# Two more weight slots for the experts, and their bias rows loaded later on the queue

## The reference

```python
def expert_block(args):
    xe, e = args
    gate = jnp.minimum(xe @ w_gate[e] + b_gate[e], SWIGLU_LIMIT)
    up = jnp.clip(xe @ w_up[e] + b_up[e], -SWIGLU_LIMIT, SWIGLU_LIMIT)
    act = (up + 1) * (gate * jax.nn.sigmoid(SWIGLU_ALPHA * gate))
    return act @ w_down[e] + b_down[e]
...
y = yb[dest] * sorted_w[:, None].astype(h.dtype)
return jax.ops.segment_sum(y, sorted_tok, num_segments=t)
```

## Time and profile before

| | us |
|---|---|
| median of three runs | 1945.78 |
| the three runs | 1941.55, 1945.78, 1946.54 |
| the profiled execution | 1945.98 |
| its span | 1944.1 |
| TensorE busy in it | 1815.6 (93%) |
| VectorE busy | 770.6 (40%) |
| ScalarE busy | 601.6 (31%) |

### The profile page before, as it was taken

The page is one execution under the profiler, slowest core; times in us unless marked ns, Lnnn a source line. Parts: engine busy times, 40 slices in busy tenths (PEclk is TensorE's granted clock), DMA queues, the critical chain, the costliest instruction groups (busy, mean ns, idle before and its releaser), DMA issues.

```text
span 1944.1 us, 24816 instructions
## 1 busy us (share of the span) xinstructions
PE 1815.6 (93%) x10349; PEld 1121.0 (58%) x10349; DVE 770.6 (40%) x1344; ACT 601.6 (31%) x1080; POOL 20.2 (1%) x59
## 2 busy tenths in 40 slices
PE   6999998999999999999999999979999999899999
PEld 4887786333333333333333333357789997779998
DVE  2654664222222213213212222244654455545554
ACT  3445564101101101101111011044554445555442
POOL 0010010000000000000000000000000000000000
PEclk9999998999999999999999999989999999999999
DMA  8655453899999999999999999954346463325550
GB/s 299 227 175 184 169 194 153 352 429 427 427 428 427 428 429 427 428 427 428 427 428 426 428 428 427 425 211 172 130 139 208 148 221 131 130 87 173 174 187 31
DMA packets 122051, 563.29 MB, mean 290 GB/s; under 512 B 7216, under 2 KB 53424, under 8 KB 97360
## 3 DMA queue, kind: packets, MB, share of 16 engines
q1 hardware_dynamic: 121104, 558.70, 71.9%
q10 hardware_dynamic: 832, 2.95, 0.4%
HBM read 560.58 MB, written 1.05 MB: 289 GB/s over the span
## 4 chain that ended last, share of the span: by engine, by line
PE 64%; DMA 28%; DVE 3%; ACT 3%; issue 1%; SPq 0%; DVEq 0%; ACTq 0%
DMA ring<-in_w_up 27%; PE ps L1020 15%; PE ps L636 12%; PE ps L637 12%; PE ps L638 12%; PE ps L1055 3%; DMA ring<-in_w_ada 1%; PE ps L648 1%; PE ps L954 1%; PE ps L971 1%; PE ps L743 1%; DVE part L1891 1%; PE ps L990 1%; PE ps L753 1%; ACT part L1370 1%
## 5 line engine op out<-in xcount | busy, mean ns | idle before, releaser
L636 PE MATMUL ps<-part,part 128*128 128x256 f32 (+2 forms) x1592 | 512.5, 322 | 9.5 <-DVE part L1891 7.9
L637 PE MATMUL ps<-part,part 128*128 128x256 f32 (+2 forms) x1592 | 504.2, 317 | 0.0
L638 PE MATMUL ps<-part,part 128*128 128x256 f32 (+2 forms) x1592 | 503.4, 316 | 0.0
L1020 PE MATMUL ps<-ring,arena 128*64 128x512 f32 x2048 | 459.5, 602 | 44.4 <-DMA ring<-in_w_up 44.1
L1891 DVE TENSOR_TENSOR part<-ring,part 128x1024 fp32r<-128x1024 f32 (+2 forms) x299 | 313.1, 1089 | 127.4 <-ACT part L1370 126.9
L1020 PEld LDWEIGHTS ps<-ring,arena 128*64 128x64 f32 x2048 | 156.1, 138 | 345.5 <-issue 345.5
L636 PEld LDWEIGHTS ps<-part,part 128*128 128x128 f32 (+1 forms) x1592 | 306.4, 192 | 40.1 <-issue 13.6
L638 PEld LDWEIGHTS ps<-part,part 128*128 128x128 f32 (+1 forms) x1592 | 305.8, 192 | 19.5
L637 PEld LDWEIGHTS ps<-part,part 128*128 128x128 f32 (+1 forms) x1592 | 306.6, 193 | 17.5
L1370 ACT ACTIVATE part<-ring 128x1024 fp32r<-128x1024 f32 (+2 forms) x299 | 271.6, 947 | 31.7 <-PE ps L638 21.6
L1888 DVE TENSOR_SCALAR arena<-ps 64x512 f32<-64x512 f32 x128 | 88.0, 688 | 390.0 <-PE ps L1020 384.5
(11 more groups left out here) (245 smaller groups left out, 996.8 us busy)
## 6 DMA issues: line engine op xcount, KB each, us to landing
ring<-in_w_gate SPq DMA_DIRECT2D x64, 2048.0 KB, 16.8
ring<-in_w_up SPq DMA_DIRECT2D x64, 2048.0 KB, 21.3
ring<-in_w_down SPq DMA_DIRECT2D x64, 2048.0 KB, 18.7
ring<-in_ffn_w_in SPq DMA_DIRECT2D x44, 1024.0 KB, 7.8
ring<-in_w_ada SPq DMA_DIRECT2D x12, 2048.0 KB, 11.3
ring<-in_ffn_w_out SPq DMA_DIRECT2D x10, 2048.0 KB, 7.9
ring<-in_w_in SPq DMA_DIRECT2D x8, 2048.0 KB, 9.2
ring<-in_a_w_in SPq DMA_DIRECT2D x6, 2048.0 KB, 12.2
```

The lines of the kernel that those rows point to most:

```text
L636: e.matmul(out, x[0], y[0], start=first, stop=False, skip_group_check=True)
L637: e.matmul(out, x[0], y[1], start=False, stop=False, skip_group_check=True)
L638: return e.matmul(out, x[1], y[0], start=False, stop=last, skip_group_check=True)
L1020: i = e.matmul(PS[p + h][CAP * r:CAP * r + CAP, :], xg[:, k0 + k, :], W(("moe_" + "gu"[r], ex, k0))[:, k, 512 * h:512 * h + 512], start=False,
```

## The change

The ring gets two more slots, 6 and 7, which only the experts use. They are no part of `ring`: each is 4096 columns of stage b's arena (columns 8192 to 16383), where stage a has places 0 to 3 of `a_wp`. They are free once piece 49 is used, which `rel` now says for `("tiles", 6)` and `("tiles", 7)`. All tiles of the experts take the eight slots in turn, in the order 4, 0, 3, 5, 2, 1, 6, 7, so each takes the slot of the tile eight back in the list. The first six tiles keep their slots and events.

Stage b's other tiles are laid anew to make room: `xg` and `S` lie where `h2` was, `aT` and `PwT` behind `wT`, and the 64-row `gus` of even and odd experts lie in the same columns, even in partitions 0 to 63 and odd in 64 to 127 (with the matching corner of the identity for the turn). `brow` now lies where stage a has `a.va`; so its four DMAs come behind the load of `w_oa`, after a wait for `s_pv.of(7)`, the last reader of `a.va`. The dense path fills `h3` from `htok` by other transposes.

```diff
--- before.py
+++ after.py
@@ -212,13 +212,14 @@
 
         loads, load_at = [], {}
         turn = itertools.count()
-        in_slot, user = [0] * NSLOT, [None] * NSLOT
+        in_slot, user = [0] * (NSLOT + 2), [None] * (NSLOT + 2)
+        more = []
 
         def plan(key, k, n, pairs_of, slot=None):
 
             if slot is None:
                 slot = (0, 3, 2, 1)[next(turn) % 4]
-            ap = ringt[:, slot, 0:k * n].rearrange("p (k n) -> p k n", k=k)
+            ap = (ringt[:, slot, 0:k * n] if slot < NSLOT else more[slot - NSLOT][:, 0:k * n]).rearrange("p (k n) -> p k n", k=k)
             pairs = pairs_of(ap)
             in_slot[slot] += 16 * len(pairs)
             loads.append((key, pairs, slot, user[slot]))
@@ -254,15 +255,7 @@
                 plan_cols(key[0:2], A["w_out"][0], 0, D, 4 * key[1], 4, key[2])
             else:
                 plan_rows(("moe_g", 0, 0), A["w_gate"][0][0], 0, key[2])
-        for ex in range(NE):
-            for k0, slots in ((0, (4, 0)), (4, (3, 5))):
-                if (ex, k0) != (0, 0):
-                    plan_rows(("moe_g", ex, k0), A["w_gate"][0][ex], k0, slots[0])
-                plan_rows(("moe_u", ex, k0), A["w_up"][0][ex], k0, slots[1])
-            for k0, slot in ((0, 2), (4, 1)):
-                plan_rows(("moe_d", ex, k0), A["w_down"][0][ex], k0, slot)
-
-        s_slot = [signal(f"slot{i}_loaded", 16) for i in range(NSLOT)]
+        s_slot = [signal(f"slot{i}_loaded", 16) for i in range(NSLOT + 2)]
         s_used = signal("weights_used")
 
         def W(key):
@@ -391,31 +384,47 @@
         lay()
         b = Box()
         b.htok = alloc3(2, D)
-        b.wT, b.mT = alloc(T, NE), alloc(T, NE)
-        b.cnt, b.posT = alloc(T, NE), alloc(T, NE)
-        b.most = alloc(NE, 1)
-        b.flag = alloc(4, 1).bitcast(I32)[:, 0:1]
+        b.wT = alloc(T, NE)
+        b.aT = [alloc3(KT, CAP) for _ in range(2)]
+        b.PwT = [alloc(T) for _ in range(2)]
         at[0] = 4096
         b.h2, b.xtok = alloc3(KT, T), alloc(512)
         b.gm, b.gm2 = alloc(D), alloc(512)
+        assert at[0] == 8192
+        more += [alloc(SLOT), alloc(SLOT)]
+        mark = at[0]
+        gus = alloc(3 * D).rearrange("p (r n) -> p r n", r=3)
+        b.gus = [gus[CAP * i:CAP * i + CAP, :, :] for i in range(2)]
+        b.yg = [alloc(512) for _ in range(2)]
+        at[0] = mark + 4608
+        b.brow = alloc(512)
+        b.most = alloc(NE, 1)
+        b.flag = alloc(4, 1).bitcast(I32)[:, 0:1]
+        at[0] = mark
+        b.mT, b.cnt, b.posT = alloc(T, NE), alloc(T, NE), alloc(T, NE)
+        at[0] = mark
+        b.h3, b.scr, b.wb = alloc3(KT, T), [alloc(512) for _ in range(4)], [alloc(T), alloc(T)]
+        at[0] = 4096
+        b.xg = [alloc3(KT, CAP) for _ in range(2)]
+        b.S = [alloc(6 * CAP) for _ in range(2)]
+        b.ac = b.h2
+        at[0] = mark + 4608 + 512 + 36
         b.Y = [[PS[2 * q + h] for h in range(2)] for q in range(2)]
         small_at[0] = 0
         b.gm1 = tiny(8)
         b.L, b.E, b.G, b.Q, b.R = ([tiny(NE) for _ in range(2)] for _ in range(5))
         b.m8, b.s = [tiny(8) for _ in range(2)], [tiny(4) for _ in range(2)]
         b.posK = tiny(64).rearrange("p (q e) -> p q e", q=2)
-        mark = at[0]
-        b.xg, b.aT = [alloc3(KT, CAP) for _ in range(2)], [alloc3(KT, CAP) for _ in range(2)]
-        b.yg, b.PwT = [alloc(512) for _ in range(2)], [alloc(T) for _ in range(2)]
-        b.S = [alloc(6 * CAP) for _ in range(2)]
-        at[0] = mark + 10 * T + 4 * 512
-        b.h3 = at[1][:, at[0]:at[0] + KT * T].rearrange("p (k n) -> p k n", k=KT)
-        b.gus = [alloc3(3, D, CAP) for _ in range(2)]
-        b.brow = alloc(512)
-        at[0] = mark
-        b.ac, b.wb = alloc3(KT, T), [alloc(T), alloc(T)]
-        b.scr = [alloc(512) for _ in range(4)]
-        b.mb = [b.scr[i // 2][:, T * (i % 2):T * (i % 2) + T] for i in range(8)]
+        order = itertools.cycle((4, 0, 3, 5, 2, 1, 6, 7))
+        next(order)
+        user[6], user[7] = ("tiles", 6), ("tiles", 7)
+        for ex in range(NE):
+            for k0 in (0, 4):
+                if (ex, k0) != (0, 0):
+                    plan_rows(("moe_g", ex, k0), A["w_gate"][0][ex], k0, next(order))
+                plan_rows(("moe_u", ex, k0), A["w_up"][0][ex], k0, next(order))
+            for k0 in (0, 4):
+                plan_rows(("moe_d", ex, k0), A["w_down"][0][ex], k0, next(order))
 
         s_logit, s_pick, s_e, s_pickT, s_pickTe = (signal(n) for n in ("router_logits", "router_steps", "router_exp", "picks_turned", "picks_evicted"))
         s_flag, s_posn, s_posK, s_most = signal("flag_ready"), signal("places_turned"), signal("places_evicted"), signal("counts_ready")
@@ -592,7 +601,8 @@
             if kind == "ada":
                 return [s_ada.of(key[1])]
             if kind == "tiles":
-                return {3: [s_merged.of(1, 1)], 4: [s_piece.of("a", 35)], 5: [s_mt.of("a", 1)]}[key[1]]
+                return {3: [s_merged.of(1, 1)], 4: [s_piece.of("a", 35)], 5: [s_mt.of("a", 1)],
+                        6: [s_piece.of("a", 49)], 7: [s_piece.of("a", 49)]}[key[1]]
             if kind in ("in", "o", "out"):
                 return [s_wlo.of("a", max(t for t, x in enumerate(a_pieces) if x[0] == key))]
             if kind in ("moe_g", "moe_u"):
@@ -608,8 +618,8 @@
                     e.wait_ge(*event)
                 for to, src in pairs:
                     e.dma_start(to, src).then_inc(s_slot[slot].sem, 16)
-                if key == ("in", "gb1"):
-                    e.wait_ge(*s_kn.of(9))
+                if key == ("o", "oa"):
+                    e.wait_ge(*s_pv.of(7))
                     for r, n in enumerate(("b_gate", "b_up")):
                         for h in range(2):
                             at = 32 * (2 * r + h)
@@ -999,7 +1009,7 @@
                     p = 6 if ex % 2 == 0 else 4
                     e.wait_ge(*s_act.of(ex, h))
                     for j in range(4 * h, 4 * h + 4):
-                        i = e.transpose(PS[p][:, CAP * j:CAP * j + CAP], b.gus[ex % 2][:, 0, 128 * j:128 * j + 128], C("ident", CAP, CAP))
+                        i = e.transpose(PS[p][:, CAP * j:CAP * j + CAP], b.gus[ex % 2][:, 0, 128 * j:128 * j + 128], C("ident")[CAP * (ex % 2):CAP * (ex % 2) + CAP, CAP * (ex % 2):CAP * (ex % 2) + CAP])
                     i.then_inc(*s_at.up(ex, h))
 
                 gather(0)
@@ -1065,10 +1075,9 @@
                     if n:
                         e.wait_ge(*s_dwbe.of("h", n - 1))
                     for j in range(2):
-                        for x in range(4):
-                            i = e.matmul(PS[5][32 * x:32 * x + 32, 256 * j:256 * j + 256], in_fours(C("ident"))[:, (2 * n + j) % 4, :],
-                                         b.h2[:, 4 * (n // 2) + x, :], start=j == 0, stop=True, skip_group_check=True,
-                                         tile_position=(0, 32 * x))
+                        at = 128 * (2 * n + j)
+                        for q in range(2):
+                            i = e.transpose(PS[5][:, T * j + 128 * q:T * j + 128 * q + 128], b.htok[:, q, at:at + 128], C("ident"))
                     i.then_inc(*s_dwb.up("h", n))
                 e.wait_ge(*s_dwbe.of("h", 3))
                 for ex in range(NE):
```

## The result

Six runs of each kernel on one chip: the changed kernel has a median of **1933.84 us** (1930.32 to 1935.64), the kernel before 1943.66 us (1941.20 to 1946.54). The ratio is **0.9947**, with a 95% interval of 0.9933 to 0.9962, that is 7.4 to 13.0 us less. Forecast were 1936.0 us and 9.85 us less; the 1936.0 was counted from a median of three runs, 1945.78, and the six lie 2.1 us lower. The profiled execution took 1933.47 us, span 1931.6, at a mean TensorE clock of 0.983.

The account below looks back on a forecast made before the run. The prediction took DMA bandwidth in the experts' stage, 428 GB/s, as the bound: 1945.98 - 9.85 + 0 (bias rows) + 0 (new places) = 1936.1, for the median 1936.0 us, with an 8-in-10 range of 1931 to 1941.

Parts of the forecast that it names:

- the whole stream of the experts: Experts' weight loads: two tiles loaded in the idle stretch before 345.83 end the stream 9.85 us earlier.
- bandwidth against slots: Experts' loop: 22 us landings read as a full queue, so bound by bandwidth and not by few slots.
- the share of 1.01: DMA share from 525 to 1235 us at 428 GB/s, taken to show no room in the queue.
- The issue of the two tiles: End of stage a: expert 1's first two tiles issued about 312.4, landed about 323, 22 us before 345.83.
- TensorE's waits: Experts: waits for w_up fall from 44.1 to about 34 us, 23 to about 18, first in expert 9.
- The bias rows: Four DMAs moved behind w_oa: between nothing and 0.6 us of queue time, taken as 0.
- the new places: Odd experts' activations in partitions 64 to 127: at most 0.8 us per odd expert, taken as 0.
- Behind the experts: From stage c's first load on, the same program 9.85 us earlier; sooner issue of the next slabs gives nothing.
- nothing would come of it: Rival 1: stream's gain given back or the two loads come too late; 1946, with half lost 1941; chance 0.10.
- the loop was bound by its slots: Rival 2: eight slots let experts run at TensorE's 27.44 us, 57 us less, 1889 us; chance 0.03.
- a longer queue is slower: Rival 3: up to two more tiles underway lower the DMA rate; at 415 GB/s 16 us slower, 1962; chance 0.04.

Follow-up runs that it names:

- layout alone: Changed kernel with the new tile places and later bias rows but the six slots and order of before; 1942.58 us, 0.999 of the kernel before.
- bias alone: Kernel before with only the four bias DMAs and their wait moved behind the load of w_oa; 1943.68 us, 0.9996.
- hold before: Kernel before, with stage c's third load and those behind it held until stage c's first piece is used; 1944.52 us, 0.9992.
- six, with eight slots (free late): Changed kernel with all eight slots, slots 6 and 7 released only when expert 0's first half is used; 1943.34 us, 0.9995 of the kernel before.
- second trace: Changed kernel, unedited, run once more beside the second run of the hold; 1934.10 us, 0.9937 of the kernel before.
- one slot: Changed kernel with only slot 6 added, seven slots in the order 4, 0, 3, 5, 2, 1, 6; 1942.62 us, 0.9982 of the kernel before.
- the loss of five: Changed kernel's layout with five slots only (4, 0, 3, 5, 2); 1958.04 us, 1.006 of the kernel before, 11.7 us more.
- the second hold: Changed kernel with stage c's third load and later ones held until its first piece is used, second run; 1934.28 us, 0.9944 of the kernel before.
- the hold's first run: Changed kernel with stage c's third load and later ones held until its first piece is used, first run; 1930.9 us, 0.9916 of the kernel before.

## Why the prediction was right

**The step that carried it.** "So the whole stream of the experts ends two tiles earlier: 2 x 4.93." The streams of all twelve traces:

| tiles loaded before the first release | stream, us |
|---|---|
| five | 916.36 |
| six (four kernels: before, layout alone, bias alone, hold before) | 910.97, 913.07, 911.33, 910.25; mean 911.4 |
| six, with eight slots (free late) | 910.34 |
| seven | 906.64 |
| eight (five executions of three kernels) | 901.57, 901.96, 902.07, 901.91, 901.68; mean 901.8 |

From five to eight it is (916.36 - 901.8) / 3 = 4.85 us per tile, against 4.93 forecast; from six to eight 911.4 - 901.8 = 9.6 against 9.85. The second row of six shows that it is the place in time and not the slot that pays. The choice of bandwidth against slots, made from the share of 1.01 in the earlier trace rows, was the right reading.

**The issue of the two tiles.** Forecast for 312.4 into an empty queue, found at 313.22 and 313.59. They landed in 12.5 us instead of 10.6, at 326 instead of 323, still 20 us before the first release: a slack that cost nothing.

**TensorE's waits.** Here a detail was wrong. "TensorE's waits fall from 44.1 to about 34 us and from 23 to about 18", the first of them in expert 9 at 596 us. Found in the changed kernel:

```profile
PE ps L1030 <- DMA ring<-in_w_up: 30.0, 18, 2.7
PE ps L1030 <- DMA arena<-in_w_up: 12.2, 8, 2.7
```

42.2 us and 26 waits, three of them short ones of a first half. The forecast left out that TensorE is not equally fast in every expert. TensorE's timeline of before, and the stretch around one block of 32 matmuls:

```profile
606.36 7.09 PE L1020 MATMUL ps<-ring,arena 128*64 128x512 f32 x32 [1.70 <-DMA ring<-in_w_up]
636.48 8.79 PE L1020 MATMUL ps<-ring,arena 128*64 128x512 f32 x32 [2.46 <-DMA ring<-in_w_up]
658.75 14.32 PE L1020 MATMUL ps<-ring,arena 128*64 128x512 f32 x64
```

```profile
636.40:646.00 9.60, 9.52 (x36) 3.67 (x38) 3.79 (x5) 0.63 (x1) 0.00 (x0) 0.82 1.01 427
```

Behind a wait of 2.46 us the block takes 8.79 us instead of 7.09, in a stretch with a granted clock of 0.82 (1.00 from 606.3 to 615.0 us, around the block before). The next expert then waits for nothing: its 64 matmuls run through. The 1.7 us went into the slower block and not into a wait, and the DMA's period is no longer for it. Before has four such blocks, and four of its 27 experts from 5 to 31 are without a wait; the changed kernel's trace has one such block. Its second trace has five, and there the waits are 34.3 us, 18 times: as forecast. With 1.7 us added for every slow block, before has 44.1 + 6.8 = 50.9 us and the changed kernel 42.2 + 1.7 = 43.9 and 34.3 + 8.5 = 42.8: the fall is 7 to 8 us and not 9.85. That the second trace meets the forecast is luck in the number of slow blocks. A period loses 29.36 - 27.44 = 1.92 us, where 2.11 was forecast, and a typical row shows 1.70 of it; where the other 0.2 goes is open. The first wait came one expert early, and barely:

```profile
568.33 7.09 PE L1030 MATMUL ps<-ring,arena 128*64 128x512 f32 x32 [0.30 <-DMA ring<-in_w_up]
```

0.30 us in expert 8. The tile had been forecast with 1.2 us to spare (9.85 less 2.3 + 3 x 2.11); but the stream gave 0.45 less than forecast and began 0.86 later, and together that is more. The forecast of the time did not rest on this number.

**The bias rows and the new places, both at 0.** The bias rows: 0.9996, the interval from 3.5 us gained to 1.9 lost; their one cost in the trace, 0.6 us at `w_oa`, was as worked out. The places: the layout alone loses nothing.

**Behind the experts.** "From there on the program is the same, only earlier." The time bears this out within its interval, the traces do so less well. From the down matmuls to the first split matmul the old layout took 27.7 and 27.4 us (before, bias alone), the new one 24.8, 24.4, 24.5, 24.7 and 23.5. Both kernels of the old layout have a second stand-still of 2.33 us after two matmuls of L954 (the hold in the kernel before has 1.68), and none of the nine traces of the new layout has one: their 16 matmuls run through in 3.4 to 3.8 us, where before takes 6.46 (1289.37 to 1295.83) for the same 16. Of the 4.2 us of the tail that is 2.7; the other 1.5 are the first wait, 4.98 against 3.46, which in the changed kernel's second trace is 4.62. The second stand-still ends behind a code packet, as shown above; that the new layout's code has the border between two packets elsewhere is inferred from that. It would explain both why the layout alone had a ratio of 0.999 and why the repeat of the changed kernel gave 12.2 us and not 9.85. So the 0 for the new places may hide a small gain; no run isolated it in the time, and the layout's interval holds zero.

**The rivals.** That nothing would come of it falls by the ratio, that the loop was bound by its slots by the unchanged period ((1256.93 - 488.94) / 26 = 29.54 us per expert before, (1248.39 - 568.33) / 23 = 29.57 after), and that a longer queue is slower by 427 GB/s with two more tiles in it.

**The size.** By the medians of the first comparison the change brought 1943.66 - 1933.84 = 9.8 us; by its ratio 10.3, by that of the repeat 12.2. The 12.5 us of the profiled pair are 9.4 of the stream and 4.2 of the tail, less 1.1 at the start and the end. The mechanism of the forecast is borne out by the stream, 9.6 us over nine traces; that the medians of the first comparison come within 0.1 us of 9.85 is luck, as the tail was not in the sum.

## What to carry to other kernels

A ring deeper than the bandwidth needs was worth here the bytes that it let the kernel load while the DMA engines would stand idle, divided by the bandwidth (4.85 us per tile against 4.93): count the tiles moved into the idle stretch, not the slots. Where the DMA share is full, time to landing measures the queue's length, and from five to eight slots the period did not change. A sum of waits is no fixed store to subtract from: in a stage bound by DMA a slower block of TensorE shortens it and costs nothing. When the order of slots changes, look at who gets them last: the loads of the next stage may be handed a slot that comes free late, which here took back part of the gain of one slot and doubled the loss of five. A branch that met full DMA queues waited here for its code: look for one where an engine stands still and the view names nobody.

## What was not expected of the hardware

**A stand-still that the view gives no cause for.** Behind the branch at the end of the experts TensorE stood for 3.5 to 5.3 us (and in the old layout for 2.3 more) while weight loads filled the queues. The branch itself took 4.6 to 6.2 us there, and 3.3 to 3.7 in the three traces with fewer loads, in which DVE ended the wait. The packets of the code queue show why: 16 KB that begin 0.9 to 1.0 us behind the branch when the queues are empty and 2.1 to 3.7 us when they are not. Most of it lies over work of DVE and ACT that is due anyway, so TensorE starts 0.3 to 2.1 us later than it would otherwise at the first place.

**Executions of one kernel fall in two groups.** The six runs of before are 1941.20, 1941.55, 1941.55 and 1945.78, 1945.90, 1946.54. In the traces one thing varies in the same measure. Over 312 to 335 us, the router, the granted clock was 0.67 to 0.71 in before, the hold in it, after and its repeat, with first releases at 345.8 to 347.7, and 0.78 in six others, among them the second hold; those had the release at 341.8 to 344.6. Two don't fit as well (0.74 with a release at 347.1, 0.80 with 345.5). The same stretch in the changed kernel's trace and in the second hold's:

```profile
312.00:335.00 23.00, 16.82 (x85) 13.62 (x83) 9.98 (x46) 9.04 (x23) 0.00 (x0) 0.69 0.46 183
```

```profile
312.00:335.00 23.00, 15.88 (x95) 10.72 (x93) 9.99 (x46) 10.98 (x27) 0.00 (x0) 0.78 0.46 183
```

That is a stretch partly at 1.2 and partly at 2.4 GHz, in which TensorE is busy for 16 to 17 of the 23 us, and some 3 us between the two. It was not tested, and it isn't the whole: the hold in the kernel before has 0.68 and a release at 346.31 and yet 1940.08 us, and the stretch from stage c's first split matmul to the end varies too, from 645.3 us there to 649.9. One more execution, of the hold's first run, took 7696.59 us and is left out of its ratio; nothing shows why.
